# Identity transposes on TensorE ahead of the loop over expert items

## The reference, cut to what matters

```python
probs = jax.nn.softmax((ht @ router).astype(F32), axis=-1)
top_p, top_i = lax.top_k(probs, TOP_K)                 # 2 of 8 experts a row
top_p = top_p / jnp.sum(top_p, axis=-1, keepdims=True)
...
for e in range(N_EXPERTS):
    out = out + gates[:, e:e + 1] * swiglu(ht, w_gate[e], w_up[e], w_down[e])
```

## Time and the profile before

| | |
|---|---|
| median of 3 runs | 2937.83 us (2930.48 to 2938.72) |
| the profiled execution | 2927.05 us |
| its span, first to last instruction | 2925.3 us |
| TensorE, busy share of the span | 92% |
| mean granted TensorE clock, share of full speed | 0.961 |
| loop over the items, TensorE's first to last matmul of it | about 1138.7 to 1779.9 us |

### The profile page before, as it was taken

The page is one execution under the profiler, slowest core; times in us unless marked ns, Lnnn a source line. Parts: engine busy times, 40 slices in busy tenths (PEclk is TensorE's granted clock), DMA queues, the critical chain, the costliest instruction groups (busy, mean ns, idle before and its releaser), DMA issues. The chain is left out here.

```text
span 2925.3 us, 54871 instructions
## 1 busy us (share of the span) xinstructions
PE 2702.9 (92%) x22883; PEld 2112.8 (72%) x22883; DVE 1576.0 (54%) x1934; ACT 1193.2 (41%) x1517; POOL 320.8 (11%) x356
## 2 busy tenths in 40 slices
PE   8999899999999987999999998987789999999998
PEld 6676678888767665777787776843677777778887
DVE  6647354343664655656666666356635544454453
ACT  5544242122454434555555554244314433433232
POOL 5022000000202210111001111022210000000002
PEclk9999899999999997999999998998989999999999
DMA  4200234233320015777777776311004331434232
GB/s 134 71 9 3 58 108 117 77 91 85 98 65 9 3 51 196 250 249 250 265 239 246 255 251 220 87 44 50 7 3 130 94 108 65 111 84 120 74 103 62
DMA packets 351955, 332.30 MB, mean 114 GB/s; under 512 B 17273, under 2 KB 269525, under 8 KB 351605
## 3 DMA queue, kind: packets, MB, share of 16 engines
q1 hardware_dynamic: 348101, 317.76, 35.0%
q0 software_dynamic: 3392, 11.14, 1.1%
q10 hardware_dynamic: 240, 0.07, 0.0%
HBM read 317.41 MB, written 11.53 MB: 112 GB/s over the span
## 5 line engine op out<-in xcount | busy, mean ns | idle before, releaser
L2913 DVE TENSOR_TENSOR experts_w_lo<-experts_raw,experts_w_hi 128x2048 fp32r<-128x2048 f32 (+1 forms) x162 | 336.0, 2080 | 225.1 <-ACT experts_w_hi L2870 210.2
L2870 ACT ACTIVATE experts_w_hi<-experts_raw 128x2048 fp32r<-128x2048 f32 (+1 forms) x162 | 282.1, 1749 | 225.0 <-DMA experts_raw<-in_moe_down 92.1
L3069 PE MATMUL experts_psum<-experts_w_hi,experts_xg_lo 128*128 128x512 f32 x384 | 162.8, 424 | 30.8 <-DVE experts_w_lo L2913 16.5
L1380 PE MATMUL proj_psum<-keep_act_hi,proj_w_lo 128*128 128x512 f32 x384 | 164.5, 428 | 15.1 <-DVE keep_act_lo L290 11.2
L3071 PE MATMUL experts_psum<-experts_w_hi,experts_xg_hi 128*128 128x512 f32 x384 | 157.1, 409 | 0.0
L3070 PE MATMUL experts_psum<-experts_w_lo,experts_xg_hi 128*128 128x512 f32 x384 | 156.7, 408 | 0.0
L1382 PE MATMUL proj_psum<-keep_act_hi,proj_w_hi 128*128 128x512 f32 x384 | 155.1, 404 | 0.0
L1381 PE MATMUL proj_psum<-keep_act_lo,proj_w_hi 128*128 128x512 f32 x384 | 154.7, 403 | 0.0
L689 PE MATMUL conv_ffn_psum<-keep_act_hi,conv_ffn_w_lo 128*128 128x512 f32 x352 | 140.6, 400 | 5.0 <-DVE keep_act_lo L290 4.9
L689 PE MATMUL ffn_psum<-keep_act_hi,ffn_w_lo 128*128 128x512 f32 x352 | 140.5, 399 | 4.9 <-DVE keep_act_lo L290 4.9
L691 PE MATMUL conv_ffn_psum<-keep_act_hi,conv_ffn_w_hi 128*128 128x512 f32 x352 | 139.9, 397 | 0.0
(11 more groups left out here) (789 smaller groups left out, 6581.7 us busy)
## 6 DMA issues: line engine op xcount, KB each, us to landing
experts_raw<-in_moe_gate SPq DMA_DIRECT2D x50, 1024.0 KB, 6.4
experts_raw<-in_moe_up SPq DMA_DIRECT2D x48, 1024.0 KB, 7.1
experts_raw<-in_moe_down SPq DMA_DIRECT2D x64, 768.0 KB, 6.1
conv_ffn_raw<-in_w_ffn_in SPq DMA_DIRECT2D x43, 512.0 KB, 4.9
proj_raw<-in_w_in SPq DMA_DIRECT2D x18, 768.0 KB, 4.3
ffn_raw<-in_ffn_up SPq DMA_DIRECT2D x22, 512.0 KB, 5.2
ffn_raw<-in_ffn_down SPq DMA_DIRECT2D x16, 704.0 KB, 5.6
conv_ffn_raw<-in_w_ffn_out SPq DMA_DIRECT2D x16, 704.0 KB, 5.7
```

The source lines that it names most:

```text
L1380: pe.matmul(out, lo, m.act_hi[:, x, :], start=x == 0, stop=False)
L2870: act.activation(w_hi[v % 2][:, s], raw[ring][:, 0:n], ACT.Copy).then_inc(rounded, 1)
L2913: dve.tensor_tensor(w_lo[v % 2][:, s], raw[(2 * v + q) % RING][:, 0:n], w_hi[v % 2][:, s].bitcast(F32), ALU.subtract).then_inc(split, 1)
L3069: pe.matmul(out, lhs[1][:, first + k, :], w_hi[slot][:, cols], start=begin and k == 0, stop=False)
```

## The change

A helper `turn_identity` is added, which transposes the 128 x 128 identity into a PSUM region n times, with no wait and no count. It is called 8 times ahead of `list_slots(0)` and 40 times ahead of `turn_rows(0)`. The target is the first 128 columns of PSUM bank 7, which the first item's down unit writes anew before anyone reads it. Each transpose is a weight load and a matmul, so 96 instructions are added to TensorE's program ahead of its loop, and all of TensorE's instructions behind them lie 96 further on in it. No other engine's program changes.

```diff
+def turn_identity(m, pe, out, n):
+
+    for _ in range(n):
+        pe.transpose(out, m.ident[:, :], m.ident[:, :])
...
             pe.nop().then_inc(h_turned, 1)
             pe.nop().then_inc(silu_done, 1)
+            turn_identity(m, pe, ps[:, 7, 0:P], 8)
             list_slots(0)
+            turn_identity(m, pe, ps[:, 7, 0:P], 40)
             turn_rows(0)
             with pe.Fori(0, items(pe)) as i:
```

## The result

The changed kernel runs in 2901.82 us, median of 4 runs (2899.32 to 2902.22), against 2936.3 us, median of 4 runs of the kernel before: a ratio of 0.9884, 95% interval 0.9867 to 0.9901. The forecast was 2901. The profiled execution took 2899.32 us with a span of 2897.5.

A forecast was written before the change was run, and what follows sets the result against it. TensorE, busy 92% of the span, was taken to stand idle and then run slow at loop returns, refetching its program. -29.6 - 12.2 + 4.1 + 0.6 = -37.1 us on 2937.8 gave 2901; range 2890 to 2940, likeliest 2892 to 2912.

The forecast's parts named there:

- The returns are fetches of a block that was dropped: Item loop's seven returns: TensorE idles 3.7 to 5.4 us each, 29.8 us in all, refetching program blocks it didn't keep.
- The idle time and the low clock, -29.6 and -12.2: Loop returns: the idle time goes, -29.6 us, and the 1.2 GHz clock behind it goes too, -12.2 us.
- What is late next, +4.1: Behind the seven returns: TensorE waits for the second half of unit 0's `w_lo`, mean 0.6 us each, +4.1 us.
- The start, +0.6: Ahead of the loop: eight transposes delay the list and so unit 1, +0.6 us; the 40 fill a wait, costed at 0.
- Where the loop lies: TensorE's loop in 256-instruction blocks: touches eight before; 96 instructions more leave seven, eight with the one asked in advance.
- x: Piece of the loop in its first 256-instruction block in the kernel before: 50 to 93 instructions, near 64.
- y: Piece of the loop in its last 256-instruction block in the kernel before: 85 to 128 instructions, near 114.
- Code behind the loop, costed at nothing: No term for shifted code behind the loop; small losses at the start or there, over 0.3%, had chance 0.02.
- The rival on the other side: Loop returns: blocks not kept and start just ahead of a border, two fetches in series, +25 us, 2963; chance 0.04.
- The one in between (supply takes most): Loop returns: blocks kept, but saturated DMA brings weights late, 2 us idle each; 2923, range 2912 to 2926; chance 0.12.

The follow-up runs named there:

- shift 60: Against the kernel before: 30 identity transposes ahead of the rows, none ahead of the list, so 60 instructions more ahead of the loop; 2902.47 us, one run.
- shift 64: The last version: changed kernel with 32 transposes ahead of the rows, none ahead of the list, 64 small ones behind the loop; 2895.76 us, ratio 0.9859.
- 48: Against the kernel before: 24 transposes ahead of the rows, none ahead of the list, so 48 instructions more ahead of the loop; 2969.41 us, one run.
- 192: Changed kernel plus 48 small transposes (96 instructions) ahead of the rows, 192 more instructions ahead of the loop than in the kernel before; 2940.0 us, one run.
- 256: Changed kernel plus 80 small transposes (160 instructions) ahead of the rows, so a whole block more than the kernel before; 2943.13 us, ratio 1.0024.

## Why the prediction was right, step by step

**The returns are fetches of a block that was dropped.** Right. It is shown from both sides: with seven blocks touched (shifts 60, 64, 96) no packet comes for the loop after the first pass, with eight (0, 48, 192, 256) nine come from each return to the next, whatever instructions make the shift (48 and 192 were run once each, 60 too). I had left open between three and nine blocks for what TensorE keeps; seven and the one asked in advance are kept, eight and one are not, so it is eight, if the one in advance counts. The Trainium skill, "Runtime: NRT & Kernel Launch", section "Instruction fetch mechanics", gives 128 KiB for TensorE and says that the memory is only two lines (beside which it names 32 KiB, its figure for most engines); the first agrees with the runs, the second doesn't: by it the packets would have stayed at 184, and 122 came.

**The idle time and the low clock, -29.6 and -12.2.** Right. Both are gone in full; the clock stays at 1.00 through all joints.

**What is late next, +4.1.** Right in place and size. From the first matmul of unit 0 to the thirteenth an undisturbed pass has 2.90 us; behind the seven returns it took 0.5, 0.3, 1.0, 0.9, 0.5, 0.3 and 0.5 us more, 4.1 in all. The clock did not fall behind them. The three terms together were -37.7 us for the loop, and it became 36.6 us shorter; the rest are three further waits for DVE of 0.2, 0.45 and 0.6 us, two of them at the start of unit 1, which I had taken to be just in time. The size is not fixed from run to run: the changed kernel run again beside the last version lost 3.5 us there in place of 4.1.

**The start, +0.6.** Unit 1 starts 0.5 us later on the clock of the trace. The 40 transposes took 7.5 us of my 7.7. The eight ahead of the list took 1.9 us and delayed it by 0.5, as forecast: DVE's picks begin at 1123.15 in this trace, 0.7 us sooner than before, and the list follows them after 1.7 us, where it was 1.2 before. But it doesn't show at unit 1. Without any transposes ahead of the list (shifts 48, 60 and 64) unit 1 starts 25.4 to 25.7 us behind the picks, in the three traces of the changed kernel 25.2 to 25.5, in the kernel before 24.3. What adds the 1 us is open.

**Where the loop lies.** I had x between 50 and 93, near 64; it is 59. My count of a pass was three too small: the records of the trace list 39 waits, register instructions and branches in it and not 36, so a pass is 1717 instructions and x + y = 181. I had y near 114; it is 122. The shift of 96 then leaves 37 instructions behind the border at the start and 38 ahead of the one at the end. By this count any shift from about 60 to 134 should do; 60, 64 and 96 were run.

**Code behind the loop, costed at nothing.** This failed. I named "all code is shifted too" only as a small chance. It cost 5.5 + 3.0 us in the profiled pair and, by the means over the kernels of each place, 86.6 - 83.3 = 3.3 us in the chunk stage and about 1.7 in the scan, 5 us in all. With it the sum would have been -32 instead of -37; measured were -34.5 between the medians (-34.8 and -32.1 on the two chips where the changed kernel was run again). The loop's gain, 1 us less than I summed, goes the same way. So the forecast of 2901 is closer than its terms deserve, and that part is luck: it lies in the start that I subtracted from. The profiled pair alone gave 2890 by my sum and measured 2899; the kernel before ranges from 2929 to 2949 over all its runs, which is wider than this term, and its profiled execution was 9 us under its median.

**The rival on the other side.** Its mechanism is real and its price was too low. I asked for a start less than about 20 instructions ahead of a border and gave 7 x 3.6 = +25 us; at 11 ahead the loop became 31.9 us longer. The fetches themselves cost no more than I gave: the seven second gaps are 23.2 us. What the price left out is the clock, at 0.94 over that loop against 0.97 before: TensorE's busy time for the same matmuls rose from 610.4 to 620.8 us.

**The one in between (supply takes most).** Wrong here: the DMA share at the joint stays about 1, and still each return loses only 0.3 to 1.0 us. It isn't far off, though: at the first return alone, the kernel with shift 60 waits 2.2 us for that half and the one with shift 64 1.8, with no fall of the clock.

What stays open: why the 96-place is worse for the chunk stage than 192 or 0. That it waits for blocks of the program more is shown; that the borders fall into bursts of short matmuls there, as at 2052.86 above, and elsewhere into pauses wasn't followed border by border. Whether the eight includes the block asked in advance wasn't tried with a longer or shorter loop body.

## What to carry to other kernels

A long unrolled loop body on one engine has a place, not only a length: count the packets of the program queue in one pass, and if there are any in the second pass, the loop doesn't stay in the engine, and an "issue" gap at the return with a low clock behind it is its price. When a body's length is within one block of what is kept, shift it by a few dozen cheap instructions put where the engine waits anyway, try several shifts, and look at the stages behind the loop as well, because they move with it. An "issue" gap in the middle of a run of matmuls can be the same thing at a block border: look for a program packet that starts 2.1 to 3.0 us ahead of its end, as here. The branch instruction's own duration, 4.0 to 5.6 us against 0.2, tells it most directly.

## What the runs showed that was not expected

Twelve instructions decide some 67 us: 2902.5 us at a shift of 60 and 2969.4 at 48, one run each, on two chips; against the kernel before on the same chip it is 33 us faster and 37 slower. And straight-line code depends on its place too: a stage of some 5400 short instructions took 81 to 88 us with nothing changed in it but where its 256-blocks begin, up to 3 us of which one and the same place shows by itself.
